# Two transformer blocks on one core: the opening modulation computed by halves of the features, its column chunks in the order 0, 2, 1, 3

## What is computed

```
sh_a, sc_a, ... = split(silu(c) @ ada_w + ada_b, 6)
csh_a, csc_a, ... = split(silu(c_ctx) @ ada_w + ada_b, 6)
h_lat = rmsnorm(x,   norm1_g) * (1 + sc_a)  + sh_a
h_ctx = rmsnorm(ctx, norm1_g) * (1 + csc_a) + csh_a
pl, pc = h_lat @ w_in, h_ctx @ w_in     # then a gated recurrence of 8 heads, attention, ...
```

## Time and profile before

| | |
|---|---|
| median of 3 runs | 3117.27 us (3116.19 to 3119.1) |
| the profiled execution | 3123.25 us |
| its span, first to last instruction | 3121.4 us |
| TensorE busy | 2990.8 us, 96% of the span |
| VectorE busy | 1501.0 us, 48% |
| ScalarE busy | 718.6 us, 23% |
| mean granted TensorE clock | 0.985 of full speed |

### The profile page before, as it was taken

One profiled execution on the slowest core, in us unless ns is written; L12 is line 12 of the kernel. 1 busy time (PEld: TensorE's weight loads), 2 busy tenths in 40 slices (PEclk: granted clock), 3 DMA queues, 4 the chain that ended last, 5 costly groups with the idle time before them and its releaser, 6 DMA issues.

```text
span 3121.4 us, 36906 instructions
## 1 busy us (share of the span) xinstructions
PE 2990.8 (96%) x14926; PEld 2208.3 (71%) x14926; DVE 1501.0 (48%) x2448; ACT 718.6 (23%) x1363; POOL 14.6 (0%) x28
## 2 busy tenths in 40 slices
PE   7999999999999999979999999999999998999998
PEld 5888888868855888854444444468888856788887
DVE  3676666726576445551101114355554426655545
ACT  3344334321176110020000013322000015300001
POOL 0000000000000000000000000000000000000000
PEclk8999999999999999989999999999999999999999
DMA  5343344241200122249999991102222211122221
GB/s 229 124 193 143 142 169 188 89 173 69 96 14 8 71 96 81 108 162 388 421 422 422 422 399 58 67 28 81 81 81 96 94 58 53 55 81 81 83 107 54
DMA packets 65417, 451.78 MB, mean 145 GB/s; under 512 B 7328, under 2 KB 9520, under 8 KB 12144
## 3 DMA queue, kind: packets, MB, share of 16 engines
q1 hardware_dynamic: 63056, 441.28, 35.5%
q0 software_dynamic: 1488, 6.06, 0.6%
q10 hardware_dynamic: 720, 2.29, 0.2%
HBM read 445.41 MB, written 2.10 MB: 143 GB/s over the span
## 4 chain that ended last, share of the span: by engine, by line
PE 86%; DMA 5%; DVE 5%; ACT 2%; DVEq 1%; issue 1%; SPq 0%; ACTq 0%
PE PS L231 79%; DMA ring<-stream 4%; PE PS L1662 1%; PE PS L1547 1%; DVE arena L1612 1%; PE PS L1645 1%; DVE stat L1671 1%; DMA hT<-stream 1%; PE PS L2363 1%; DMA arena<-x 1%; PE PS L2343 1%; DVE PS L2688 0%; ACT arena L1565 0%; PE PS L886 0%; PE PS L2346 0%
## 5 line engine op out<-in xcount | busy, mean ns | idle before, releaser
L231 PE MATMUL PS<-arena 128*128 128x256 f32 (+3 forms) x4960 | 985.3, 389 | 6.6 <-DVE arena L1142 1.7
L231 PEld LDWEIGHTS PS<-arena 128*128 128x128 f32 (+1 forms) x4960 | 744.9, 183 | 234.7 <-issue 152.6
L231 PE MATMUL PS<-arena,ring 128*128 128x256 f32 (+1 forms) x1992 | 467.0, 390 | 0.4 <-issue 0.4
L231 PE MATMUL PS<-hT,ring 128*128 128x256 f32 (+1 forms) x1504 | 413.2, 430 | 23.2 <-ACT hT L326 11.5
L231 PEld LDWEIGHTS PS<-arena,ring 128*128 128x128 f32 x1992 | 377.7, 190 | 74.6 <-issue 26.3
L231 PEld LDWEIGHTS PS<-hT,ring 128*128 128x128 f32 x1504 | 291.5, 195 | 131.1 <-issue 87.2
L231 PE MATMUL PS<-xT,arena 128*128 128x256 f32 x1056 | 232.0, 379 | 0.0
L231 PEld LDWEIGHTS PS<-xT,arena 128*128 128x128 f32 x1056 | 200.6, 190 | 28.1 <-issue 1.0
L231 PE MATMUL PS<-ring,arena 128*32 128x512 f32 (+3 forms) x1088 | 199.8, 594 | 11.8 <-issue 6.4
L231 PE MATMUL PS<-hT,arena 128*128 128x256 f32 (+1 forms) x864 | 195.2, 442 | 1.3 <-DMA hT<-stream 1.3
L2127 DVE TENSOR_TENSOR arena<-arena,PS 128x512 f32<-128x512 f32 x16 | 11.0, 687 | 370.1 <-PE PS L231 370.1
(11 more groups left out here) (309 smaller groups left out, 2862.3 us busy)
## 6 DMA issues: line engine op xcount, KB each, us to landing
ring<-stream SPq DMA_DIRECT2D x281, 1024.0 KB, 6.9
arena<-stream SPq DMA_DIRECT2D x98, 1024.0 KB, 18.9
hT<-stream SPq DMA_DIRECT2D x32, 1024.0 KB, 18.8
arena<-stream SPq DMA_DIRECT2D x8, 512.0 KB, 5.0
arena<-x ACTq DMA_DIRECT2D x4, 512.0 KB, 15.2
xT<-stream SPq DMA_DIRECT2D x2, 1024.0 KB, 20.8
arena<-arena POOLq DMA_DIRECT2D x16, 128.0 KB, 2.6
xT<-x POOLq DMA_DIRECT2D x1, 2048.0 KB, 10.5
```

The costliest lines, as they stand in the source:

```text
L231: ins = nc.tensor.matmul(out_, lhsT, rhs, start=start, stop=stop_, **kw)
```

## The change

1. `EARLY`: chunks stream and are computed in the order 0, 2, 1, 3, so that after the second the shift and the scale of feature tiles 0 to 3 are there.
2. TensorE's order in the opening: each `select` comes right behind its chunk, and the matmul with ones behind the third chunk instead of ahead of it.
3. Biases and scales are made per half of the features (`start_mods`): 4 small VectorE instructions for the first half ahead of the norm, 4 for the second behind it. The selected rows of the two halves go to banks 4 and 5.
4. ScalarE's order: three chunk copies, the reciprocal root, shift of tiles 0 to 3, the fourth copy, shift of tiles 4 to 7.
5. The block differences and the weight sums of product 0 alternate on VectorE in the order in which the parts need them (`turned_sum`, `sums_dve` with `which`).
6. ScalarE, before the first head: `context_act(0, 2)` ahead of `second_decay(0)`.

```diff
-    order = [("c", 0, 0), ("c", 1, 1), ("c", 2, 2), ("c", 3, 3), ("F", 0, 0), ("v", 0, None),
+    order = [("c", 0, 0), ("c", 2, 1), ("c", 1, 2), ("c", 3, 3), ("F", 0, 0), ("v", 0, None),
...
             chunk(0)
+            select(0)
             chunk(1)
-            select(0)
+            select(1)
+            chunk(2)
             pe.wait_ge(n_ac, 1)
             mm(PS[:, 7, :], ones, hT[:, 0, :], True, True, n_ss)
-            chunk(2)
-            select(1)
+            select(2)
             chunk(3)
-            select(2)
             select(3)
...
             chunk_evac(act, 0)
             chunk_evac(act, 1)
+            chunk_evac(act, 2)
             scale_act(act, 0)
-            chunk_evac(act, 2)
+            act.wait_ge(mods_ok, 1)
+            norm_shift(act, 0, hT, 1, mod[:, 0:KT], range(0, KH))
             chunk_evac(act, 3)
-            act.wait_ge(mods_ok, 1)
-            norm_shift(act, 0, hT, 1, mod[:, 0:KT])
+            act.wait_ge(mods_ok, 2)
+            norm_shift(act, 0, hT, 1, mod[:, 0:KT], range(KH, KT))
...
-            norm_dve(v, 0, x0, hT)
-            v.wait_ge(ada_sel, ADA0 + 1)
+            for half in range(2):
+                start_mods(v, half)
+                if half == 0:
+                    norm_dve(v, 0, x0, hT)
+
+        def start_mods(v, half):
+
+            v.wait_ge(ada_sel, 2 * half + 3)
             v.wait_ge(in_vec, 16)
-            m3 = PS[:, 4, 0:12 * ADA0].rearrange("p (c m) -> p c m", m=3)
-            nc.vector.tensor_tensor(mod[:, 0:16], m3[:, :, 0], V[:, V_ADAB:V_ADAB + 16], ALU.add)
-            nc.vector.tensor_tensor(modc[:, :], m3[:, :, 1], V[:, V_ADAB:V_ADAB + 16], ALU.add)
-            v.drain()
-            norm_scales(0, ((modc, 8, V_N1), (mod, 8, V_N1)))
+            m3 = PS[:, 4 + half, 0:24].rearrange("p (c k m) -> p c k m", c=2, m=3)
+            groups = lambda x: x.rearrange("p (c k) -> p c k", c=2)[:, :, KH * half:KH * half + KH]
+            b = groups(V[:, V_ADAB:V_ADAB + 16])
+            nc.vector.tensor_tensor(groups(mod[:, 0:16]), m3[:, :, :, 0], b, ALU.add)
+            nc.vector.tensor_tensor(groups(modc[:, :]), m3[:, :, :, 1], b, ALU.add)
+            v.drain()
+            for r, m in enumerate((modc, mod)):
+                k0 = KH * half
+                nc.vector.scalar_tensor_tensor(gsc[:, r, k0:k0 + KH], m[:, KT + k0:KT + k0 + KH], 1.0,
+                                               V[:, V_N1 + k0:V_N1 + k0 + KH], ALU.add, ALU.mult)
             v.drain().then_inc(mods_ok, 1)
...
+            context_act(act, 0, 2)
             second_decay(act, 0)
-            context_act(act, 0, 2)
...
-            sums_dve(v, 0)
-            turned_sums(v, NM[0])
+            turned_sum(v, 0, NM[0] + KH)
+            sums_dve(v, 0, (0, 1))
+            turned_sum(v, 2, NM[0] + KT)
+            sums_dve(v, 0, (2,))
+            turned_sum(v, 1)
             last_sum_dve(v, 0)
+            turned_sum(v, 3)
```

More of the change, by code:

```diff
@@ L320, in norm_dve, with norm_shift @@
                                                    ALU.mult, ALU.mult).then_inc(n_h, 1)
-        def norm_shift(act, use, dst, row, sh, n=T):
-            for k in range(KT):
+        def norm_shift(act, use, dst, row, sh, tiles=range(KT), n=T):
+            for k in tiles:
                 act.wait_ge(n_h, NH[use] + k + 1)
@@ L475, in start_pe, with select, chunk @@
             first(pe, ada_sel)
-            def select(c):
-                pe.wait_ge(evac_done, chunk_turn(c) + 1)
+            def select(n):
+                pe.wait_ge(evac_done, G_ADA + n + 1)
                 for j in range(4):
-                    ins = nc.tensor.matmul(PS[:, 4, 12 * c + 3 * j:12 * c + 3 * j + 3],
-                                           arow[:, c % 2, j * P:(j + 1) * P], C[:, C_SEL:C_SEL + 3],
+                    ins = nc.tensor.matmul(PS[:, 4 + n // 2, 12 * (n % 2) + 3 * j:12 * (n % 2) + 3 * j + 3],
+                                           arow[:, n % 2, j * P:(j + 1) * P], C[:, C_SEL:C_SEL + 3],
                                            start=True, stop=True)
                 ins.then_inc(ada_sel, 1)
[L485 to L488, removed]
+            def chunk(n):
+                if n >= 2:
+                    pe.wait_ge(evac_done, G_ADA + n - 1)
                 for k in range(KT):
-                    q, su = k % 4, UNIT_OF["c", c] + k // 4
+                    q, su = k % 4, UNIT_OF["c", CHUNKS[n]] + k // 4
                     if q == 0:
                         unit_wait(pe, su)
-                    mm(PS[32 * q:32 * q + 32, c % 2, :], cs[:, k, :], ring[slot(su)][:, q * 512:(q + 1) * 512],
+                    mm(PS[32 * q:32 * q + 32, n % 2, :], cs[:, k, :], ring[slot(su)][:, q * 512:(q + 1) * 512],
                        k < 4, k >= 4, mm_done if k == KT - 1 else None, tile_position=(0, 32 * q))
-                if c < 3:
+                if n < 3:
                     places.append(w_pair[slot(su) // 2])
@@ L708, in corner_act, with turned_sum @@
             nc.scalar.activation(quad_out(n)[0][:, :, 0:HN], part_bank(0), func).then_inc(p_c, 1)
[L710 removed]
+        def turned_sum(v, i, ready=None):
             B = halves(hT)
[L713 to L717, removed]
[L718 to L721 removed]
+            a, b = ((B[0, 1], B[0, 0]), (B[1, 1], T_x[:, 0, :, :]), (B[1, 1], B[0, 1]), (B[1, 0], T_x[:, 1, :, :]))[i]
+            if i == 0:
+                v.wait_ge(w_pair[2], 1)
+            if ready is None:
+                v.drain()
+            else:
+                v.wait_ge(n_mod, ready)
+            nc.vector.tensor_tensor(T_x[:, i, :, :], a, b, ALU.subtract).then_inc(p_t, 1)
         def block_sums(v, x, Tt, free=(0, 0, 0, 0)):
@@ L732, in block_sums, with sums_dve @@
                 nc.vector.tensor_tensor(Tt[i], a, b, ALU.subtract).then_inc(p_t, 1)
-        def sums_dve(v, n):
+        def sums_dve(v, n, which=range(3)):
             u = quad_unit(n)
             A = weight_blocks(u)
-            v.drain()
-            unit_wait(v, u)
-            unit_wait(v, u + 1)
-            if n:
-                v.wait_ge(p_p, 7 * (n - 1) + 3)
-            nc.vector.tensor_tensor(part_sum(n, 0), A[1, 0], A[1, 1], ALU.add).then_inc(p_s, 1)
-            if n:
-                v.wait_ge(p_p, 7 * (n - 1) + 4)
-            nc.vector.tensor_tensor(part_sum(n, 1), A[0, 0], A[1, 0], ALU.subtract).then_inc(p_s, 1)
-            if n:
-                v.wait_ge(p_p, 7 * (n - 1) + 6)
-            v.drain()
-            nc.vector.tensor_tensor(part_sum(n, 2), part_sum(n, 0), A[0, 0], ALU.subtract).then_inc(p_s, 1)
+            for i in which:
+                if i == 0:
+                    v.drain()
+                    unit_wait(v, u)
+                    unit_wait(v, u + 1)
+                elif i == 2:
+                    if n:
+                        v.wait_ge(p_p, 7 * (n - 1) + 6)
+                    v.drain()
+                if n and i < 2:
+                    v.wait_ge(p_p, 7 * (n - 1) + 3 + i)
+                a, b, op = ((A[1, 0], A[1, 1], ALU.add), (A[0, 0], A[1, 0], ALU.subtract),
+                            (part_sum(n, 0), A[0, 0], ALU.subtract))[i]
+                nc.vector.tensor_tensor(part_sum(n, i), a, b, op).then_inc(p_s, 1)
         def last_sum_dve(v, n):
```

11 lines of the change are left out of this document (5 added, 6 removed).

## The result

The changed kernel took 3124.62 us (median of 20 runs, 3119.45 to 3128.5), the kernel before in the same comparison 3119.03 us (20 runs, 3116.19 to 3123.36): 5.6 us slower, ratio 1.0017 with an interval of 1.001 to 1.0023, which is 3.1 to 7.2 us. The forecast was +2.9 us and 3120.2; the measured time lies 0.6 us above the stated range. The ratio itself is within the 0.2% bound, as forecast, though its interval reaches past it, and it is on the side of the loss.

What follows compares the result with a forecast made beforehand. TensorE, busy 96% of the span, was taken to bound the kernel. The opening's +3.5 us and the first head's -0.6 us made +2.9 us, which on 3117.3 us gave 3120.2 us, range 3113.5 to 3124.

Steps and rivals of the forecast that it cites:

- What bounds it, and where the change acts: TensorE, busy 96% of the span, bounds the kernel; the change touches only the opening and the first head's start.
- The opening, +3.5 us, between -0.2 and +5.25: Start of part 1 of product 0: later because the second chunk waits behind the first select and the norm follows.
- +2.1: Opening: part 1 of product 0 starts 2.1 us later if TensorE's clock is high from the third chunk on.
- I expect the rise later than in the good case: Opening: a 0.7 us gap and short selects should delay the clock's rise; all high after the first select gives -0.2.
- the low clock lasts through the opening: Slower rival: opening +5.25, part 1 of product 0 another 0.9, head +0.1; +6.3 us in all, 3123.5 us; chance 0.2.
- The alternation, 0: VectorE's alternating sums and differences for product 0 gain 0 us, as parts 1 and 2 cover that work.
- The first head, -0.6 us: First head: earlier context copy starts part 1 sooner, but a gap ahead of the levels costs clock; ends -3.2 and +0.1.
- So the levels start at 107.45 instead of 110.65: 3.2 us are kept: First head: VectorE's operand, ready at 107.45, limits the level products, so 3.2 us of the 6.4 remain.
- 1.9 to 3.3 us are lost again: First head: idle TensorE ahead of the levels lowers the clock, as two rows behind 3.11 us showed; mean 2.6 us.
- The sum, +2.9 us: Whole kernel: opening +3.5 and first head -0.6 give +2.9 us, forecast 3120.2 us.
- since two medians of three runs that spread over 3 us are compared, about 0.5 us more: Whole time: allowance for measurement spread added to the ends of both terms, giving the range 3113.5 to 3124.
- The rule of the skill: Opening and head: clock ramp under 1% of span, varying, not to be fitted; by it all clock terms would drop.

Runs made afterwards that it cites:

- first changed execution: Changed kernel's first profiled execution, lowest of its 20 runs: part 1 of product 0 came 19.55 us behind the last two squares of x; median +5.6 us against kernel before.
- The five executions: Profiled executions of the unaltered changed kernel, one per comparison with the kernel before; the medians there were +5.6, +1.0, +2.2, +1.8 and +0.5 us.
- head alone: Kernel before with only ScalarE's last context copy moved ahead of the second decay; median -4.4 us (11 runs), ratio 0.9985 against the kernel before.
- fourth changed execution: Changed kernel, unaltered, profiled a fourth time; part 1 of product 0 came 22.72 us behind the last two squares of x; median +1.8 us against the kernel before (12 runs).
- first comparison: Changed kernel against the kernel before, 20 runs each: 3124.62 against 3119.03 us, ratio 1.0017.
- the later four: Repeated comparisons of the unaltered changed kernel with the kernel before: +1.0, +2.2, +1.8 and +0.5 us, 11 or 12 runs each.
- fifth changed execution: Changed kernel, unaltered, profiled a fifth time; part 1 of product 0 came 20.06 us behind the last two squares of x; median +0.5 us against the kernel before (11 runs).

## Why the prediction was right or wrong

**What bounds it, and where the change acts**: right as far as the landmarks reach. They find the loss and the gain in the two places named, both before H; that the rest is the same for both kernels is shown to 2 us or so, not closer.

**The opening, +3.5 us, between -0.2 and +5.25**: right, in mechanism and size. Where the clock rises by the third chunk, the working gave the norm at 35.99 and part 1 at 42.24; the first changed execution has 36.38 and 42.76, and its last two squares come 0.43 us later. The five executions have +2.6 to +5.7 over the mean of the kernel before, +3.9 on average, two of them a little past the upper end. That 3.5 came so near the average is partly luck: it was called the middle, which of +2.1 and +5.25 is 3.7 and of the stated ends 2.5, and how often the clock would rise late was a guess. The second chunk behind the first select and the last select behind the shifts are where they were said to be. "I expect the rise later than in the good case" held in two of five. The rival *the low clock lasts through the opening* is not an alternative, then, but what happens in some executions: P at 45.03 and 45.51, against its 45.39. Its further 0.9 us in part 1 did not come: part 1 took 5.72 and 5.17 us there, less than the 6.01 of before.

**The alternation, 0**: right within 0.4 us, by one execution.

**The first head, -0.6 us**: the sign was right, the size was not. Two steps failed. "So the levels start at 107.45 instead of 110.65: 3.2 us are kept" is right for the first level (107.47 in head alone), but the third has a wait of its own, for the merge of the first, 1.22 us. And "1.9 to 3.3 us are lost again", always, was wrong: behind gaps of 2.9 to 3.2 us the clock fell in 4 of the 13 executions without filler there, and it then cost 1.5 us up to H (6.39 from the first level, in the fourth changed execution, where the first has 4.89) and up to 1 us more in part 5. The two rows behind 3.11 us gaps were two falls out of two, and were read as a rule. Measured: -1.4 us from the values to H (-1.7 from P). The two mistakes pull opposite ways, 1.2 us less gained and on average some 2 us less lost, so that -0.6 came as near as it did is luck.

**The sum, +2.9 us**: the landmarks give +2.2, all runs together +1.9 by medians and +3.0 by means. The first comparison gave +5.6. What failed there is the last step, from the sum to the time and its range: "3117.3 + 2.9", with "since two medians of three runs that spread over 3 us are compared, about 0.5 us more". The measured time is 4.4 us above 3120.2. Of these 1.8 us are the base: the kernel before had 3119.03 in the first comparison and 3118.5 over all its runs, where 3117.27 was shown, and against itself it moved by up to 2 us. The other 2.7 us are the difference, 5.6 instead of 2.9. A range that allowed 2 us in place of 0.5 would have held 3124.62.

Why the first comparison came out some 3 us higher than the later four is not settled: no execution of it but one was profiled, and that one was its fastest. The clocks of its runs say a part. The mean granted clock was 0.9864 over those 20 runs and 0.9879 over the 45 later ones; among the 45, 0.001 less of it goes with 1.3 us more, so a lower clock would go with 2.0 of the 3.8 us between the two means (3124.2 and 3120.4). Where in the program it was lower, and why, no trace shows.

**The rule of the skill.** The Trainium skill (TensorE: Matmul & The Clock Gate, "Part 1: The HAM clock gate") has the ramp vary from run to run and advises against fitting it. The five executions agree on the variation (P - S from 19.55 to 22.72 for one program). Dropping the clock terms altogether would have given -3.4 us and the wrong sign, though: the low clock in the opening costs something in every execution (the first select took 1.86 or 1.87 us in all five), only not the same.

## What to carry to other kernels

Ask of each instruction that is moved behind a wait what it did with the time before: here a chunk of work that had been free, in the shadow of an input's arrival, went onto the path, with the norm behind it, and the halves that it was to serve gained less than that (3.9 against 6.1 us). Before crediting the removal of a wait, follow each later consumer separately, down to the third level product: the first was held by an operand, the third by a bank. Where the effect is a few microseconds, compare landmarks over several executions instead of spans, and give the difference of two medians the spread that the unchanged kernel shows against itself.

## What the runs showed of the hardware

- One program's TensorE clock differs from execution to execution: in the changed opening it rose before 30 us in one and at about 38 us in another, 3.2 us of difference at P.
- Behind a gap of 2.9 to 3.2 us on TensorE the clock fell in 4 of 13 executions. Their gaps were 2.96 to 3.16 us long, those of the other nine 2.88 to 2.97. In three of the four it was still up at the end of the gap and fell 1.4 to 1.5 us into the work behind it. Filling the gap with 2.75 us of matmuls on constants kept the clock up in the one execution tried.
- Filler helped here only right up to the next real work: extra matmuls that ended 4.6 us before the select left the clock to fall behind it; where they ended at most 0.7 us before it, the clock stayed up for the ten microseconds of the opening and then fell all the same, at the start of part 1 (5.33 and 5.38 us instead of 3.69), behind short selects and waits of under 1 us.
- The recorded clock can miss a fall: in the fifth changed execution it reads 1.00 from 24 to 31 us, while the first select took 1.87 us and the second chunk 3.64, the times of the low level. So durations are read beside it.
- The part of the program behind H, identical in all these kernels, lasted from 3000.0 to 3008.9 us in their single executions: a spread larger than any effect measured here at a landmark.
